# Gate table reads moved from the sync engine's queue to ScalarE's queue, two blocks ahead

## What is computed

```python
def peer(h, wq, subkeys, u_tab, v_tab):
    ...
        sc = jnp.einsum('thpd,hpkd->thpk', qry, subkeys).astype(F32)
        s1, i1 = lax.top_k(sc[:, :, 0], PEER_TOPK)
        s2, i2 = lax.top_k(sc[:, :, 1], PEER_TOPK)
        ...
        eid = e1 * PEER_NKEYS + e2
        g = jax.nn.softmax(sf, axis=-1)
        ug = jnp.take(u_tab, eid, axis=0)
        vg = jnp.take(v_tab, eid, axis=0)
        act = jax.nn.gelu(jnp.einsum('td,thkd->thk', xb, ug).astype(F32))
        return jnp.einsum('thk,thkd->td', (g * act).astype(xb.dtype), vg)
```

## Time and profile before

| | us |
|---|---|
| median of 3 runs | 4282.13 (4257.39 to 4283.33) |
| the profiled execution | 4268.13 |
| its span in the trace | 4266.4 |
| PE busy in the span | 3875.4 (91%) |
| DVE / ACT / POOL busy | 2668.1 / 1186.0 / 673.8 |

### The profile page before, as it was taken

How to read it: one execution, slowest core, us unless ns; L and a number is a source line. 1 busy time by engine, 2 the same in 40 slices (tenths; PEclk the granted TensorE clock), 3 DMA queues, 4 the chain that set the end, 5 groups by cost and what they waited for, 6 DMA issues and landing times. The chain is left out here.

```text
span 4266.4 us, 57315 instructions
## 1 busy us (share of the span) xinstructions
PE 3875.4 (91%) x21916; PEld 2052.0 (48%) x21916; DVE 2668.1 (63%) x4848; ACT 1186.0 (28%) x1708; POOL 673.8 (16%) x544
## 2 busy tenths in 40 slices
PE   5999687699968799989999997999999999999997
PEld 3676343166633544545555553344444444444443
DVE  5133111477645500989989974877778777777665
ACT  4233111144234311333334432222222222222223
POOL 0000000233101000000000002211111144444431
PEclk8999898899888899999999998999999999999999
DMA  5232541623064312899997879999999999999993
GB/s 203 94 119 78 159 127 60 234 88 100 32 233 152 113 55 86 217 241 291 300 266 227 228 217 242 274 246 246 250 248 246 223 274 286 282 281 284 268 246 120
DMA packets 985882, 846.06 MB, mean 198 GB/s; under 512 B 755026, under 2 KB 835242, under 8 KB 978219
## 3 DMA queue, kind: packets, MB, share of 16 engines
q1 hardware_dynamic: 921540, 568.86, 52.1%
q0 software_dynamic: 60112, 215.78, 15.0%
q10 hardware_dynamic: 4032, 58.72, 3.4%
HBM read 620.46 MB, written 186.31 MB: 189 GB/s over the span
## 5 line engine op out<-in xcount | busy, mean ns | idle before, releaser
L2936 PE MATMUL ex_psy<-ex_vhi,ex_wboth 128*128 128x512 f16 x3584 | 1080.2, 380 | 28.0 <-DVE ex_wboth L2795 13.2
L2904 PE MATMUL ex_psa<-h_hi,ex_uth 128*128 128x512 f16 (+1 forms) x2048 | 727.4, 355 | 43.5 <-DMA ex_utl<-ex_ulo 36.0
L2904 PE MATMUL ex_psa<-h_lo,ex_uth 128*128 128x512 f16 (+1 forms) x2048 | 726.3, 355 | 0.0
L2904 PE MATMUL ex_psa<-h_hi,ex_utl 128*128 128x512 f16 (+1 forms) x2048 | 726.1, 355 | 0.0
L2936 PE MATMUL ex_psy<-ex_vlo,ex_wboth 128*128 128x512 f16 x1792 | 681.6, 380 | 0.0
L2936 PEld LDWEIGHTS ex_psy<-ex_vhi,ex_wboth 128*128 128x128 f16 x3584 | 351.6, 98 | 457.1 <-DVE ex_wboth L2795 13.6
L2447 POOL DMA_INDIRECT ex_ug<-in_peer_u_dram,ex_idxp x128 | 154.5, 1207 | 1497.7 <-DVE ex_ug L2760 1071.5
L2756 DVE TENSOR_TENSOR ex_acc<-ex_acc,ex_psy 128x512 f32<-128x512 f32 x434 | 292.7, 683 | 153.8 <-PE ex_psy L2936 153.8
L2485 ACT ACTIVATE ex_wa<-ex_psa 128x512 f32<-128x512 f32 (+1 forms) x256 | 134.7, 542 | 677.8 <-PE ex_psa L2904 520.8
L2904 PEld LDWEIGHTS ex_psa<-h_hi,ex_uth 128*128 128x128 f16 x2048 | 201.2, 98 | 228.9 <-DMA ex_utl<-ex_ulo 40.0
L2904 PEld LDWEIGHTS ex_psa<-h_hi,ex_utl 128*128 128x128 f16 x2048 | 201.3, 98 | 190.8 <-issue 6.3
(11 more groups left out here) (388 smaller groups left out, 6124.2 us busy)
## 6 DMA issues: line engine op xcount, KB each, us to landing
ex_u<-in_peer_u_dram SPq DMA_DIRECT2D x128, 512.0 KB, 6.1
ex_v<-in_peer_v_dram SPq DMA_DIRECT2D x128, 512.0 KB, 5.6
gate_all<-rt_stage ACTq DMA_DIRECT2D x28, 2048.0 KB, 7.6
ex_gate<-gate_all SPq DMA_DIRECT2D x128, 448.0 KB
act_all<-ex_wa SPq DMA_DIRECT2D x80, 448.0 KB, 3.3
ex_wa<-act_all SPq DMA_DIRECT2D x80, 448.0 KB, 5.7
ad_w<-in_ada_w_dram SPq DMA_DIRECT2D x8, 2048.0 KB, 10.5
sh_w<-in_w_in_dram SPq DMA_DIRECT2D x10, 1024.0 KB, 8.3
```

The source lines that it names most:

```text
L2904: mm = nc.tensor.matmul(ps_a[:, at:at + e - a], x[s][:, k, :], h[:, k, a:e], start=(k == 0 and j == 0), stop=(k == KD - 1 and j == 2))
L2936: mm = nc.tensor.matmul(sum_bank(q, n), w, v_[:, a * 512:(a + 1) * 512], start=(j == 0), stop=(j == len(mms) - 1))
```

## The change

The read of the gate table becomes a helper that any engine can issue. SP issues it for blocks 0 and 1 alone, both ahead of the first load of `v`, after the same wait for the stored table. ACT issues all others: block n+2's read right behind its own wait for the gate product of block n, and ahead of the `w_hi` copy. SP's `w_done` wait is gone; ACT's was there before.

```diff
+            def load_gate(eng, eb, s):
+
+                eng.dma_start(gate[s][:, :].rearrange("p (m t) -> p m t", t=RUN), gates[eb]).then_inc(g_in[s], 16)
+
...
                             for e in range(2):
                                 sp.wait_ge(stage_stored[e], DENSE // RUN // 2 * 16)
+                            for e in range(2):
+                                load_gate(sp, block_at(0, e, False), e)
                             sp.dma_start(v[0][:, :], rows_of("peer_v", block_at(0, 0, False))).then_inc(v_in[0], 16)
-                        sp.wait_ge(w_done, n + 1)
-                        sp.dma_start(gate[s][:, :].rearrange("p (m t) -> p m t", t=RUN), gates[eb]).then_inc(g_in[s], 16)
                         if more(n, 1):
...
                         act.wait_ge(w_done, n + 3)
+                        if more(n, 2):
+                            load_gate(act, block_at(g1, b + 2, kept) if b + 2 < EB else first_of(g1 + 1, kept) + b + 2 - EB, s)
                         nc.scalar.activation(w_both[k][:, 0:DENSE], wa[s][:, :], ACT.Copy).then_inc(w_hi_done, 1)
```

## The result

| | before | after |
|---|---|---|
| median of 4 runs each, us | 4269.76 (4254.47 to 4283.33) | 4364.02 (4362.59 to 4383.02) |
| span of the profiled execution, us | 4266.4 | 4361.6 |
| PE / DVE busy, us | 3875.4 / 2668.1 | 3898.7 / 2672.2 |

A forecast was written before the change was run, and what follows sets the result against it. PE was taken as the bound, leaving at most 45.8 us of idle time plus the opening's low clock. From 4268.13 us, -1.1 (opening) and -5.5 (late stretch) gave 4261.5 us, range 4236 to 4292.

The forecast's parts named there:

- What bounds the kernel: Experts' stage: PE always busy in kept and first full groups; gain at most 45.8 us idle plus the opening's low clock.
- The opening: First blocks of the experts' stage: 3.5 us gained at block 2's product, 2.4 lost behind it, balance 1.1 us gained.
- The two terms up to block 2's product: Opening: block 0's product 7.0 us late, block 2's product 3.5 us earlier.
- The two charged stalls of 4.26 us: Opening, SP's queue: 4.26 us of issue time each for gate 1 behind gate 0 and for the first `v`.
- The term of 0.4 us a block: Opening and first kept group, block 2 to 7: ACT's issue delays `w_lo`, 6 x 0.4 = 2.4 us lost.
- What it adds in every block: 126 issues on ACT delay `w_lo` by 0.3 to 0.4 us a block, uncovered only in opening and first kept group.
- the cover: DVE's idle time, 1.9 us a kept block and 4.9 us a full-group block, was to absorb the issue's delay.
- The late stretch: Between 3960 and 4200: DVE's 23.2 us of gate waits go, 5.5 us gained at most, 0 at least.
- Rival 3: Transposes come late beside gates and gathers on three queues: 10 of 44 blocks by 2 us, +20 us, 4288; chance 0.08.
- Rival 2: ACT gets stuck at the issue, say 4.26 us a block: 184 us slower, 4452 us; chance 0.03.
- what would show it: Trace signs: no gate waits but block 0's, PE busy throughout; hidden late transfers would show as grown `ex_ug` or `ex_utl` waits.
- a time of 4268: Whole kernel, by the skill page: spreading DMAs over engines adds no bandwidth and saves sequencer issue time alone, so 4268.

The follow-up runs named there:

- act_copy_first: The changed kernel with ACT's two instructions exchanged, the `w_hi` copy first and then the gate read: 4255.84 us, 0.9987 of before.
- sp_early: The changed kernel with all gate reads on SP's queue, gate n+1 issued in block n ahead of the transposes: 4251.83 us, 0.9986 of before.
- copy_delay: The kernel before with a spare 128x384 copy on ACT ahead of every `w_hi` copy, no transfer moved: 4263.20 us, 1.0007 of before.
- sp_delay: `sp_early_v` with ACT's spare 128x384 copy ahead of the `w_hi` copy in every block: 4247.34 us, 0.9917 of before.
- small_read_delay: `copy_first_delay` with ACT's gate reads cut to the first of 28 pieces, 16 KB of 448: 4250.54 us, 0.9931 of before.
- copy_first_delay: `act_copy_first` with the spare 128x384 copy of `copy_delay` ahead of the `w_hi` copy: 4369.12 us, 1.0265 of before.
- act_rows: The changed kernel with the gate read as 128 rows of 3584 bytes, not 3584 pieces of 128 (other gate values): 4402.15 us, 1.0337 of before.
- act_mid: The changed kernel with ACT reading gate n+1 in block n between its two gelus: 4261.07 us, 1.0002 of before.
- sp_early_v: `sp_early` with the order v 0, gate 0, v 1, gate 1 in the opening: 4246.85 us, 0.9968 of before.
- sp_behind_v: The changed kernel with all reads on SP's queue, gate n+1 right behind v n+1, in the opening too: 4249.74 us, 0.9959 of before.
- after_short_dots3: The changed kernel with all three dots of each gather batch on 512 of 1024 columns: 4261.04 us, 0.9977 of before.

## Why the prediction was wrong

**What bounds the kernel.** Right for before: PE at 570.00 of 570 us. What it left out is how near the next bound was. The loop from weighted sum through POOL and gather to the dot does not appear in the chain of before's full groups, since PE is always busy there.

**The opening.** The two terms up to block 2's product held. Block 0's product came 7.5 us after SP's first issue before and 13.85 after, 6.3 us late where 7.0 were predicted, waiting for gelu as forecast. Block 2's came after 48.7 us and now after 43.0, 5.7 us gained where 3.5 were predicted, without a wait. SP's issues that answer those of the earlier trace rows are:

```profile
2585.59 4.38 SPq L2340 DMA_DIRECT2D ex_gate<-gate_all  x2
2590.03 3.99 SPq L2410 DMA_DIRECT2D ex_v<-in_peer_v_dram  x1
```

The two charged stalls of 4.26 us measured about 3.8 and 3.99 us. DVE's products that answer (blocks 0 and 2), and `w_lo` of block 2:

```profile
2599.44 1.09 DVE L2796 SCALAR_TENSOR_TENSOR ex_wa<-ex_wa,ex_gate 128x896 f32<-128x896 f32 x1 [11.46 <-ACT ex_wa L2489]
...
2628.58 1.08 DVE L2796 SCALAR_TENSOR_TENSOR ex_wa<-ex_wa,ex_gate 128x896 f32<-128x896 f32 x1
...
2635.23 1.09 DVE L2801 TENSOR_TENSOR ex_wboth<-ex_wa,ex_wboth 128x896 f16<-128x896 f32 x1 [4.43 <-ACT ex_wboth L2550]
```

With the kept groups the sum was -1.1 us predicted and +1.2 measured, so 6.9 us were lost behind block 2's product and not 2.4. The term of 0.4 us a block left out a stuck issue: ACT's read behind block 2's product took 4.51 us, and `w_lo` waited 4.43 for the copy behind it. With the copy ahead of the read (`act_copy_first`), or the reads on SP (`sp_early`), opening and kept groups take 797.2 and 797.1 us, about 8 less than in the kernel before.

**What it adds in every block: the step that failed.** The size was right for the median block: the copy starts 0.43 us later, and `w_lo` of a kept block, which followed `v_lo` at once in the earlier trace rows, has 0.45 us of idle time ahead of it where 0.3 to 0.4 were predicted:

```profile
3005.77 1.09 DVE L2801 TENSOR_TENSOR ex_wboth<-ex_wa,ex_wboth 128x896 f16<-128x896 f32 x1 [0.45 <-ACT ex_wboth L2550]
```

The term that failed is the cover. "In the full groups DVE is idle ... 4.9 us for each of about 31 blocks" was taken as cover. That idle time is not free: the gathers are issued only when the weighted sums are done, so 0.4 us less of it brings them 0.4 us nearer to the transposes (a lead of 5.2 and 2.6 us in place of 5.6 and 3.0). What came of it is the 72 us of PE's idle time and the 29 us of the lower clock above, where this term stood at nothing. The delay has no price that adds up by block: it costs nothing at the median in `copy_delay`, `sp_delay` and `small_read_delay`, and it makes all of the 113 us between `act_copy_first` and `copy_first_delay` (4255.84 and 4369.12). In the kept groups, which have no transposes, the same argument from idle time held.

**The late stretch: the second step that failed.** "Nothing else in SP's order gets worse" looked at the order alone. On SP's queue the read had been issued behind the transposes; now it left beside them. The predicted 5.5 us are there where the slow pattern stays away: `sp_early` and `act_copy_first` have PE busy 240.00 of 240 us behind 3960.

**The rivals.** Rival 3 named the right place, transposes that land late beside gates and gathers. It took the maximum of the earlier trace rows, 17.9 us, for a rare case. Over all blocks the median still moved little,

```profile
DMA to landing us min/median/max: 3.1/5.4/19.7
```

but in the full groups it is 16.5 us. And it looked at PE's wait for the transposes, which was only 2.5 us behind 3390; the price was paid on DVE, for the gathers, and came to PE through `add`. At "10 of 44 blocks by 2 us" it was put at a fifth of what came. Rival 2's stuck issues did happen, up to 11.18 us, and one of them held `w_lo` up in the opening, but the median is 0.379 us and `act_rows` loses more without them. The section on what would show it did name the signs that came (waits of DVE for `ex_ug`, PE idle); it gave them too little chance.

**More queues.** The Trainium skill's page "DMA: Bandwidth & Descriptors", section "Rules for kernel authors", says that issuing DMAs from several engines saves only the time of issue. The runs agree: `act_mid`, with its reads on ACT's queue and no loss, moves 279 GB/s between 3390 and 3960, the kernel before 277. By it the prediction worked out a time of 4268, no change, and that did not follow; `copy_first_delay` and `small_read_delay` differ in the traffic on ACT's queue alone, and by 119 us.

## What to carry to other kernels

Idle time of an engine is cover only if nothing behind it depends on when its work is done. Before one spends it, follow what it releases (here DVE to POOL to DMA to DVE), add up that loop and see which transfers it would meet if it came later. Try a transfer that would run beside DMA transposes on the transposes' own queue first, ahead of them (`sp_early_v`) or behind them (`sp_behind_v`): neither order lost time here. If it must be issued by an engine with work of its own, put the issue behind that work. Here that exchange of two instructions was worth 2.5%.

## What was not expected of the hardware

- Two causes that cost nothing singly (1.0007 and 0.9987) cost 2.65% together: the stage has two ways to run, blocks of 18.1 us on PE's pace and of 21.4 us in the slow pattern. The changed kernel did not get back to the first; with the read cut to 16 KB the stage was back after one long block.
- The second transpose and the gathers take 16.5 and 13.2 us to land when they start together with the 448 KB read beside them on ACT's queue, against 4.2 and 6.3 us in the kernel before. With the read cut to 16 KB they take 5.0 and 6.4, and with plain transfers of the same tiles 4.6 and 6.0.
- When PE idles in every block, its work takes longer as well: 29 us more for as many matmuls, at a granted clock of 0.97 in place of 1.00.
- A DMA issue that stands behind an ACTIVATE in ACT's program leaves 0.01 to 0.16 us after the start of that ACTIVATE (`act_copy_first`); an ACTIVATE behind a DMA issue starts 0.42 to 0.46 us after it began, and 10.36 and 11.23 us after it where it was stuck. With rows of 128 bytes such an issue took up to 14.01 us (`after_short_dots3`), with rows of 3584 bytes at most 0.402.
